# Attention input of a two-block transformer kernel: one joint stage with five gate tiles, three gate tiles in quarters

## The chip, the cores and the metric

The kernel runs on one core of a Trainium2 chip. Its engines each follow their own instruction list and meet only at semaphores: TensorE multiplies matrices (PE in the rows, PEld its weight loads), VectorE (DVE) and ScalarE (ACT) do elementwise work, GpSimd (POOL) a little, and SyncE (SP) issues the DMAs. A matmul writes into one of eight banks of PSUM (`ps`, "banks" in the rows); everything else lies in SBUF. The metric is device microseconds of one execution, median of the runs. Lower is better.

## The reference, cut to what matters

The function is a first block (two attentions, a mixture of 16384 experts) followed by a second block on 272 rows (16 meta tokens and 256 tokens), first attention, then a gated delta rule. The change touches only the attention of the second block. Its core is:

```python
def attention_mixer(h, norm_w, w_in, q_norm_w, k_norm_w, sinks, w_out):
    u = rms_norm(h, norm_w) @ w_in
    q, k, v, gate = jnp.split(u, [1024, 1152, 1280], axis=-1)   # then 1024 columns of gate
    q = rms_norm(q.reshape(B, L, 16, 64), q_norm_w)
    k = rms_norm(k.reshape(B, L, 2, 64), k_norm_w)
    v = v.reshape(B, L, 2, 64)
    o = banded_sink_attention(q, k, v, sinks)   # window 128, plus the 16 meta keys, plus a sink logit
    return (o * jax.nn.silu(gate)) @ w_out
```

All is float32. There are 272 rows (L), 16 query heads and 2 key heads of 64.

## The kernel before, in words

Weights are tiles of 128 x 1024 floats (512 KB), eight 128 x 128 chunks each, that stream through a ring of four slots. The list `plan` fixes their order; `load_tiles` lets SyncE load the next one as soon as VectorE has done with the tile four back. Each tile is split: ScalarE rounds it to a high part (`make_high`, L175), VectorE subtracts to get the low part (`make_low`, L187). There are two buffers of each, so parts of a tile can be made only when the tile two back is used. `tile_T` (L222, L226) multiplies a tile: 16 matmuls with the high part and 8 with the low part, all into one bank, 128 x 272. The names `early` and `end_early` mean that the first two tiles of a group are split in the stage before.

A stage is an `nc.Block` in which every engine has its own list. At its end all engines meet. Around the change the stages of `second_block` are, in order:

1. `project_T`: 11 tiles of the attention input, heads on partitions. Tiles 0 to 7 are the queries, 8 and 9 the keys, 10 the values. VectorE copies each from its bank.
2. `value_rows_stage`: three transposes give the values with tokens on partitions. The first two gate tiles are split here.
3. `head_norm_stage`: ScalarE squares the ten tiles, TensorE adds the squares per head ("gather", L1449), VectorE and ScalarE form the inverse root (L1462, L1443, and `newton`, L1408 to L1416), TensorE spreads it over the rows again ("spread", L1456), VectorE multiplies (L1764).
4. `meta_attention_stage`: the 16 meta rows attend to each other. It is one chain: scores (L1667), peaks, exponentials, scaling, turning (L1672), values (L1678), copy (L1705).
5. `sink_attention_stage`: 16 units (a unit is two heads of 128 query rows; units 0 to 7 have two key tiles, units 8 to 15 three). In step u TensorE does the scores of unit u+2 (L1512), then in steps 0 to 7 a whole gate tile, then the values of unit u-1 (L1539), then turns the weights of unit u (L1524). Per unit VectorE adds the bias, finds peaks and scales (L1567 to L1591), ScalarE exponentiates (L1608, L1611) and copies the turned weights (L1619, L1622), the gate (L1640) and the output (L1630). Two steps after the last gate tile ScalarE applies Silu to all eight gates at once (L1647).

The order is written out by hand: the Python loops emit each engine's list, and only the semaphores set when an instruction may start. After these comes the output projection (L2784) and the delta rule.

## Time and profile before

| what | value |
|---|---|
| median of 3 runs | 1849.21 us (1848.17 to 1852.97) |
| the profiled execution | 1853.29 us, its span 1851.5 us, mean granted clock 0.947 |
| TensorE busy | 1679.9 us, 91% of the span |
| VectorE, ScalarE busy | 65%, 48% |
| DMA | 124 GB/s on average |
| projection to output projection | 1210.50 to 1371.49 us of the span |

The span is what the trace covers; the profiled execution is 1.8 us longer. A row of the timeline gives the start, the length, the engine, the line, the operation and its tiles, how many instructions were merged, and in brackets the idle time ahead of the first and what ended it. Merged instructions of a row may overlap with the next row at their ends, so the distance of two starts tells more than a length. A matmul of plain float32 counts as two instructions on TensorE (x2). "PEclk" is the clock that TensorE was granted, in parts of 2.4 GHz.

### The profile page before, as it was taken

Reading aid. Unit: us, or ns where it says so; the run is one execution under the profiler, and the core shown is the slowest. Engines: PE = TensorE matmul, PEld = TensorE weight load, DVE = VectorE, ACT = ScalarE, POOL = GpSimd, SP = SyncE. Lnnn points to the kernel's source line nnn. Section 1 sums busy time; section 2 is a strip of 40 time slices with the busy share of each in tenths; the row PEclk is TensorE's granted clock in tenths of the full one; section 3 lists DMA queues with packets and bytes.
Section 4 is the critical chain, followed back from the end, with each engine's and each line's share of the span. In section 5 each row is a group of like instructions: output and inputs, shape, how many; then the busy total and the mean of one; then the engine's idle time right before and its main releaser. Section 6 shows DMA issues by size and latency. Waiting matters only on the chain. (4 is left out here: it accounts for less than half of the span.)

```text
span 1851.5 us, 34628 instructions
## 1 busy us (share of the span) xinstructions
PE 1679.9 (91%) x13270; PEld 1497.3 (81%) x13270; DVE 1199.9 (65%) x2104; ACT 894.8 (48%) x1568; POOL 69.9 (4%) x35
## 2 busy tenths in 40 slices
PE   5989988899999999989999999687987999899969
PEld 5978777899999999988888888584656888788857
DVE  3456654479989799996666666544644657655555
ACT  3335544244554666665666666432633644233323
POOL 0000000000000000000000000000000333100000
PEclk9979998999999999999999999896978999999989
DMA  5532143454555433335666666431112444200004
GB/s 174 170 123 81 57 137 119 145 170 159 182 172 176 129 115 115 115 115 184 193 192 194 192 194 193 135 126 36 56 46 68 149 155 141 92 3 3 3 17 143
DMA packets 63079, 230.05 MB, mean 124 GB/s; under 512 B 7008, under 2 KB 7264, under 8 KB 62832
## 3 DMA queue, kind: packets, MB, share of 16 engines
q1 hardware_dynamic: 62960, 228.39, 38.9%
q8 instruction: 83, 1.36, 0.3%
q14 instruction: 36, 0.29, 0.1%
HBM read 227.32 MB, written 1.05 MB: 123 GB/s over the span
## 5 line engine op out<-in xcount | busy, mean ns | idle before, releaser
L974 DVE TENSOR_TENSOR tile_low<-weights,tile_high 128x1024 fp32r<-128x1024 f32 x252 | 307.2, 1222 | 146.6 <-ACT tile_high L964 142.8
L964 ACT ACTIVATE tile_high<-weights 128x1024 fp32r<-128x1024 f32 x252 | 268.2, 1064 | 136.2 <-issue 136.2
L175 ACT ACTIVATE tile_high<-weights 128x1024 fp32r<-128x1024 f32 x169 | 177.7, 1057 | 273.8 <-PE banks L222 107.6
L187 DVE TENSOR_TENSOR tile_low<-weights,tile_high 128x1024 fp32r<-128x1024 f32 x146 | 179.7, 1237 | 187.9 <-ACT tile_high L175 152.2
L222 PE MATMUL banks<-parts,tile_high 128*128 128x272 f32 (+1 forms) x1904 | 268.1, 295 | 14.6 <-PEq L262 6.8
L1026 PE MATMUL banks<-parts,tile_high 128*128 128x256 f32 x2048 | 272.4, 286 | 7.1 <-PEq L900 7.1
L222 PEld LDWEIGHTS banks<-parts,tile_high 128*128 128x128 f32 x1904 | 249.2, 195 | 32.1 <-issue 25.1
L1026 PEld LDWEIGHTS banks<-parts,tile_high 128*128 128x128 f32 x2048 | 256.9, 193 | 7.3 <-issue 7.3
L1311 PE MATMUL banks<-tile_high,parts 128*128 128x512 f32 x1024 | 254.6, 391 | 4.6 <-ACT parts L1291 4.6
L1311 PEld LDWEIGHTS banks<-tile_high,parts 128*128 128x128 f32 x1024 | 193.3, 189 | 45.0 <-issue 4.8
L1031 PE MATMUL banks<-parts,tile_low 128*128 128x256 f32 x1024 | 148.6, 288 | 21.6 <-DVE tile_low L974 21.5
L1031 PEld LDWEIGHTS banks<-parts,tile_low 128*128 128x128 f32 x1024 | 132.8, 193 | 28.3 <-DVE tile_low L974 27.9
L226 PE MATMUL banks<-parts,tile_low 128*128 128x272 f32 (+1 forms) x952 | 138.5, 288 | 0.9 <-DVE tile_low L187 0.9
L1311 PE MATMUL banks<-tile_low,parts 128*128 128x512 f32 x512 | 137.5, 390 | 0.0
L226 PEld LDWEIGHTS banks<-parts,tile_low 128*128 128x128 f32 x952 | 127.5, 193 | 1.1 <-DVE tile_low L187 1.1
L1311 PEld LDWEIGHTS banks<-tile_low,parts 128*128 128x128 f32 x512 | 96.7, 189 | 20.2
L1102 ACT ACTIVATE rows<-rows,kept 128x128 f32<-128x128 f32 x256 | 80.5, 391 | 62.7 <-DVE rows L1181 62.7
L1081 ACT ACTIVATE big<-banks 128x256 f32 (+1 forms) x79 | 52.7, 667 | 120.2 <-PE banks L1031 120.2
L1291 ACT ACTIVATE parts<-big 128x256 fp32r (+1 forms) x128 | 88.4, 692 | 4.3 <-PEq L1007 4.3
L2784 PE MATMUL banks<-tile_high,parts 128*128 128x512 f32 (+1 forms) x288 | 77.6, 417 | 8.7 <-ACT tile_high L175 6.6
L1328 DVE TENSOR_TENSOR parts<-big,parts 128x256 fp32r<-128x256 f32 x128 | 81.1, 635 | 1.0 <-ACT parts L1291 1.0
L1181 DVE TENSOR_TENSOR rows<-const,kept 128x512 f32<-128x512 f32 x128 | 80.8, 685 | 0.0
(341 smaller groups left out, 2000.4 us busy)
## 6 DMA issues: line engine op xcount, KB each, us to landing
weights<-in_peer_u SPq DMA_DIRECT2D x128, 512.0 KB, 3.6
weights<-in_peer_v SPq DMA_DIRECT2D x128, 512.0 KB, 3.5
weights<-in_dn_in SPq DMA_DIRECT2D x49, 512.0 KB, 3.6
weights<-in_in_t SPq DMA_DIRECT2D x19, 512.0 KB, 3.6
weights<-in_attn_t SPq DMA_DIRECT2D x19, 512.0 KB, 3.6
weights<-in_in_m SPq DMA_DIRECT2D x16, 512.0 KB, 3.6
weights<-in_wq SPq DMA_DIRECT2D x16, 512.0 KB, 3.5
weights<-in_dn_out SPq DMA_DIRECT2D x16, 512.0 KB, 3.6
```

The lines of the kernel that those rows point to most:

```text
L175: k.nc.scalar.activation(k.high[:, m % 2, :], k.ring.view(n), ACT.Copy).then_inc(*k.high_made.up())
L187: unit.tensor_tensor(k.low[:, m % 2, :], k.ring.view(n), k.high[:, m % 2, :].bitcast(F32), ALU.subtract).then_inc(*k.low_made[engine].up())
L222: ins = nc.tensor.matmul(out, high[:, c, :], rhs(c)[part], start=part + c == 0, stop=False)
L226: ins = nc.tensor.matmul(out, low[:, c, :], rhs(c)[0], start=False, stop=c == chunks - 1)
L964: k.nc.scalar.activation(k.high[:, (s + j) % 2, :], k.ring.buf[:, j % RING, :], ACT.Copy).then_inc(k.high_made.sem, 1)
L974: k.nc.vector.tensor_tensor(k.low[:, (s + j) % 2, :], k.ring.buf[:, j % RING, :], k.high[:, (s + j) % 2, :].bitcast(F32), ALU.subtract).th ...
L1026: ins = nc.tensor.matmul(ps[:, bank, 0:S], high[:, c, :], x[:, c, :], start=part + c == 0, stop=False)
L1031: ins = nc.tensor.matmul(ps[:, bank, 0:S], low[:, c, :], k.pair(S)[0][:, c, :], start=False, stop=c == KC - 1)
L1181: return nc.vector.tensor_tensor(out, iota.unsqueeze(1).broadcast_to([P, Q, NKEY]), k.chosenT[:, o, Q * g:Q * g + Q].unsqueeze(2).broadcas ...
L1291: nc.scalar.activation(stage[:, j % STAGES, :], c_of(i, j), ACT.Copy).then_inc(staged.sem, 1)
L1311: ins = nc.tensor.matmul(ps[:, 2 * tt + half, :], c[:, j % STAGES, tt * P:tt * P + P], v[:, half, :], start=head and j + part == 0, stop=t ...
L1328: nc.vector.tensor_tensor(stage_low[:, j % STAGES, :], c_of(i, j), stage[:, j % STAGES, :].bitcast(F32), ALU.subtract).then_inc(staged_low ...
```

## The change

Stages 1 to 4 become one stage, `attn_in_stage`, with 16 tiles instead of 11: the eleven of before and the first five gate tiles (`GATES_FIRST`). Four banks take the tiles in turn. The gather of head tile t follows tile t+1; the value transposes follow tile 11, the spreads tile 12, the meta scores tile 13. Spreads use two banks in turn and one matmul of full width each, from a table `picks` that VectorE writes at the start. The turning and the values of the meta attention stand after tile 15. Gates are copied by ScalarE. The remaining three gate tiles go through `tile_piece`, six matmuls of a tile at a time, one piece in each of the steps 0 to 11 of the sink attention. The split of a tile then stands at steps 5, 9 and 13, the Silu at step 14 in place of 10.

```diff
-N_ATTN = 11
+N_ATTN, GATES_FIRST = 11, 5
...
+def tile_piece(pe, k, n, out, rhs, piece, pieces):
...
+    for m in range(3 * KC * piece // pieces, 3 * KC * (piece + 1) // pieces):
+        part, c = divmod(m, KC)
+        if m == 0:
+            await_high(pe, k, n)
+        if m == 2 * KC:
+            await_low(pe, k, n)
+        ins = nc.tensor.matmul(out, (low if part == 2 else high)[:, c, :], rhs(c)[part % 2], start=m == 0,
+                               stop=m == 3 * KC - 1, skip_group_check=True)
...
+def attn_in_stage(k):
...
+            def gather(c):
+                pe.wait_ge(*squared.at(c + 1))
+                nc.tensor.matmul(ps[0:HEADS, 7, 0:L], k.c("pair")[:, 18 - 2 * c:38 - 2 * c], sq[:, c % 2, :],
+                                 start=c == 0, stop=c == V - 1).then_inc(*summed.up())
...
+            def spread(c):
+                if c == 0:
+                    pe.wait_ge(*root.at(7))
+                if c >= 2:
+                    pe.wait_ge(*applied.at(c - 1))
+                nc.tensor.matmul(ps[:, 5 + c % 2, 0:L], halves(c), r[:, 2, :], start=True, stop=True).then_inc(*wide.up())
...
+            for t in range(count):
+                if t >= 4:
+                    if t - 4 <= V:
+                        pe.wait_ge(*evacuated.at(t - 3))
+                    else:
+                        pe.wait_ge(*gated.at(t - 4 - V))
+                tile_T(pe, k, first + t, bank(t), lambda c: (high[:, c, :], low[:, c, :]))
+                if 1 <= t <= V:
+                    gather(t - 1)
+                if t == N_ATTN:
+                    turn_values()
+                if t == spread_at:
+                    for c in range(V):
+                        spread(c)
+                if t == meta_at:
+                    meta_scores()
+            meta_turn()
+            meta_values()
...
+            for t in range(-AHEAD, count):
+                if 0 <= t <= V:
+                    evacuate(t)
+                if t == spread_at:
+                    for c in range(V):
+                        finish(c)
+                if t + AHEAD < count:
+                    make_low(dve, k, first + t + AHEAD)
+                if t == norm_at:
+                    mean_squares()
+                if t == N_ATTN:
+                    dve.wait_ge(*rooted.at(1))
+                    newton(nc, dve, root, r[:, 0, :], r[:, 1, :], r[:, 2, :], r[:, 3, :])
+                    copy_values()
+                if t == meta_at:
+                    meta_peaks()
+                if t == meta_at + 1:
+                    meta_scale()
+            for n in early(k, "attn_g"):
+                make_low(dve, k, n)
+            dve.wait_ge(*meta_product.at(2))
+            done(nc.vector.tensor_copy(over.rearrange("p h n -> p (h n)"), ps[0:m, 4, 0:AH * m]))
+            dve.wait_ge(*meta_product.at(3))
+            done(nc.vector.tensor_copy(k.y2[:, :, 0:m], ps[:, 7, 0:8 * m].rearrange("p (c n) -> p c n", c=8)))
...
+            for t in range(-AHEAD, count):
+                if t + AHEAD < count:
+                    make_high(act, k, first + t + AHEAD)
...
+                if t >= N_ATTN:
+                    act.wait_ge(k.ring.used.sem, first + t + 1)
+                    nc.scalar.activation(T[:, GATE + t - N_ATTN, :], bank(t), ACT.Copy).then_inc(*gated.up())
...
+            for n in early(k, "attn_g"):
+                make_high(act, k, n)
...
-                if u < fills:
-                    if u:
-                        pe.wait_ge(*gated.at(u))
-                    tile_T(pe, k, gate_tile(u), fill, lambda c: (high[:, c, :], low[:, c, :]))
+                if u < filled:
+                    if u and u % pieces == 0:
+                        pe.wait_ge(*gated.at(u // pieces))
+                    tile_piece(pe, k, gate_tile(u // pieces), fill, lambda c: (high[:, c, :], low[:, c, :]), u % pieces, pieces)
```

How the instruction lists move, at three places. First TensorE before, from the value transposes (L1723) through gathers (L1449), spreads (L1456) and the meta attention (L1667 to L1678) to the first scores of the sink attention (L1512):

```order
L1723 MATMUL banks<-const,big 128x128 x2
L1718 UNCONDITIONAL_BRANCH
L1445 UNCONDITIONAL_BRANCH
L1449 MATMUL banks<-big 20x272 x10
L1456 MATMUL banks<-big,const 64x272 x20
L1430 UNCONDITIONAL_BRANCH
L1663 UNCONDITIONAL_BRANCH
L1667 MATMUL banks<-big 16x16 x16
L1672 MATMUL banks<-const,rows 16x16 x16
L1678 MATMUL banks<-rows,big 64x16 x16
```

The same place now, from tile 11 on (value transposes L1477, spreads L1485, meta scores L1491, turning L1499, values L1507):

```order
L1477 MATMUL banks<-const,big 128x128 x2
L222 MATMUL banks<-parts,tile_high 128x272 x16
L226 MATMUL banks<-parts,tile_low 128x272 x8
L1485 MATMUL banks<-big 128x272 x10
L222 MATMUL banks<-parts,tile_high 128x272 x16
L226 MATMUL banks<-parts,tile_low 128x272 x8
L1491 MATMUL banks<-big 16x16 x16
L222 MATMUL banks<-parts,tile_high 128x272 x16
L226 MATMUL banks<-parts,tile_low 128x272 x8
L222 MATMUL banks<-parts,tile_high 128x272 x16
L226 MATMUL banks<-parts,tile_low 128x272 x8
L1499 MATMUL banks<-const,rows 16x16 x16
```

Four gate tiles moved in between the parts; the turning of the meta weights and their values have no tile behind them in this stage.

Second, VectorE at the end of the joint stage now: the last step of the meta scaling (L1574), the early low parts (L187), the copy of the turned weights (L1599), the copy of the meta output (L1601), and the bias of the sink attention (L1722):

```order
L1573 RECIPROCAL small<-small 16x16
L1574 TENSOR_TENSOR rows<-rows,small 16x256
L187 TENSOR_TENSOR tile_low<-weights,tile_high 128x1024 x2
L1599 COPY rows<-banks 16x256
L1601 COPY big<-banks 128x8x16
L1461 UNCONDITIONAL_BRANCH
L1712 UNCONDITIONAL_BRANCH
L1722 SCALAR_TENSOR_TENSOR big<-big,banks 128x144 x2
```

Before, the two early low parts stood ahead of the head norm, right after the value copies (L1729). Now they stand between the meta scaling and the copy that the meta values wait for.

Third, TensorE in the first steps of the sink attention before (turning L1524, scores L1512, values L1539):

```order
L222 MATMUL banks<-parts,tile_high 128x272 x16
L226 MATMUL banks<-parts,tile_low 128x272 x8
L1524 MATMUL banks<-const,big 16x128 x2
L1524 MATMUL banks<-const,big 128x128 x2
L1512 MATMUL banks<-big 128x144 x2
L222 MATMUL banks<-parts,tile_high 128x272 x16
L226 MATMUL banks<-parts,tile_low 128x272 x8
L1539 MATMUL banks<-big 64x128 x4
```

And now (piece L240, turning L1679, scores L1667, values L1694):

```order
L240 MATMUL banks<-parts,tile_high 128x272 x6
L1679 MATMUL banks<-const,big 16x128 x2
L1679 MATMUL banks<-const,big 128x128 x2
L1667 MATMUL banks<-big 128x144 x2
L240 MATMUL banks<-parts,tile_high 128x272 x6
L1694 MATMUL banks<-big 64x128 x4
```

Where 24 matmuls of a tile stood in a step, six stand.

## Rows read from the trace of the kernel before

**Rows 1.** The page, its first line.

```profile
span 1851.5 us, 34628 instructions
```

**Rows 2.** Stretches: us; busy PE, PEld, DVE, ACT, POOL; clock; DMA share, GB/s.

```profile
1260.50:1271.00 10.50, 9.33 (x40) 4.46 (x40) 5.44 (x11) 0.00 (x0) 0.00 (x0) 0.50 0.01 2
1281.00:1287.50 6.50, 6.33 (x30) 5.73 (x31) 3.56 (x16) 2.13 (x11) 0.00 (x0) 0.50 0.51 165
1342.40:1356.00 13.60, 11.87 (x45) 7.00 (x45) 6.59 (x24) 6.49 (x25) 0.00 (x0) 0.50 0.00 1
1369.80:1376.40 6.60, 4.91 (x12) 3.22 (x13) 4.00 (x6) 1.29 (x2) 0.00 (x0) 0.50 0.48 163
```

**Rows 3.** Timeline of TensorE, 1222 to 1281: start, length, idle before in brackets.

```profile
1222.57 2.16 PE L222 MATMUL banks<-parts,tile_high 128*128 128x272 f32 x16
...
1225.57 2.16 PE L222 MATMUL banks<-parts,tile_high 128*128 128x272 f32 x16
...
1244.53 0.49 PE L1723 MATMUL banks<-const,big 128*16 128x128 f32 x3 [0.80 <-PEq L329]
1248.82 7.59 PE L1449 MATMUL banks<-big 128*20 128x272 f32 x20 [3.81 <-ACT big L1441]
1260.99 9.33 PE L1456 MATMUL banks<-big,const 20*64 20x272 f32 x40 [4.58 <-DVE big L1416]
...
1275.76 0.59 PE L1672 MATMUL banks<-const,rows 16*16 16x16 f32 x16 [3.95 <-DVE rows L1701]
1276.92 3.19 PE L1678 MATMUL banks<-rows,big 16*64 16x16 f32 x32 [0.57 <-DVE rows L1703]
1281.04 2.31 PE L1512 MATMUL banks<-big 64*128 64x144 f32 x12 [0.93 <-PEq L1661]
```

**Rows 4.** Timeline of VectorE and ScalarE, 1228 to 1289.

```profile
1228.91 1.23 DVE L187 TENSOR_TENSOR tile_low<-weights,tile_high 128x1024 fp32r<-128x1024 f32 x1 [1.42 <-ACT tile_high L175]
...
1244.59 2.00 ACT L175 ACTIVATE tile_high<-weights 128x1024 fp32r<-128x1024 f32 x2 [6.71 <-PEq L329]
...
1257.37 1.84 DVE L1408 RECIPROCAL big<-big 20x272 f32<-20x272 f32 x1 [0.49 <-ACT big L1443]
...
1263.12 0.50 DVE L1764 SCALAR_TENSOR_TENSOR big<-banks,param,big 128x272 f32<-128x272 f32 x1 [0.34 <-PE banks L1456]
...
1285.34 0.50 DVE L1591 TENSOR_SCALAR big<-big,small 128x144 f32<-128x144 f32 x2
...
1288.59 0.40 ACT L1640 ACTIVATE big<-banks 128x272 f32<-128x272 f32 x1 [0.16 <-PE banks L226]
```

**Rows 5.** Timeline of TensorE in the delta input stage, gathers between tiles.

```profile
1441.09 0.63 PE L1846 MATMUL banks<-rows,big 128*16 128x272 f32 x2
...
1444.86 0.63 PE L1846 MATMUL banks<-rows,big 128*16 128x272 f32 x2
```

**Rows 6.** Timeline of TensorE in the sink attention and after it.

```profile
1306.23 2.26 PE L222 MATMUL banks<-parts,tile_high 128*128 128x272 f32 x16
...
1309.43 1.51 PE L1539 MATMUL banks<-big 16*64 16x128 f32 x8
...
1311.85 2.27 PE L222 MATMUL banks<-parts,tile_high 128*128 128x272 f32 x16
...
1333.43 1.95 PE L1539 MATMUL banks<-big 16*64 16x128 f32 x12 [0.43 <-ACT big L1622]
...
1336.07 0.73 PE L1512 MATMUL banks<-big 64*128 64x272 f32 x4
1337.23 1.95 PE L1539 MATMUL banks<-big 16*64 16x128 f32 x12 [0.43 <-ACT big L1622]
...
1344.13 3.39 PE L1539 MATMUL banks<-big 16*64 16x128 f32 x12 [3.54 <-ACT big L1622]
...
1350.04 3.39 PE L1539 MATMUL banks<-big 16*64 16x128 f32 x12
...
1371.49 5.21 PE L2784 MATMUL banks<-tile_high,parts 128*16 128x512 f32 x12 [2.19 <-ACT parts L2744]
```

More of the change, by code:

```diff
@@ L227, in tile_T @@
     tile_used(ins, k, n)
+def tile_piece(pe, k, n, out, rhs, piece, pieces):
+    nc = k.nc
+    high, low = parts(k, n, KC)
+    for m in range(3 * KC * piece // pieces, 3 * KC * (piece + 1) // pieces):
[6 more added lines that the diff above has]
+                               stop=m == 3 * KC - 1, skip_group_check=True)
+        if m == 2 * KC - 1:
+            ins.then_inc(*k.high_used.up())
+    if piece == pieces - 1:
+        tile_used(ins, k, n)
 def tile_used(ins, k, n):
@@ L1417, in newton @@
     dve.wait_ge(*sig.last())
-def head_norm_stage(k, chunks, heads, gather, spread, scale, eps, finish):
-    nc, ps, xs = k.nc, k.ps, chunks
-    n = len(xs)
-    squared, summed, vec, rooted, wide, applied = k.start("head_squared", "head_summed", "head_vector",
-                                                          "head_rooted", "head_spread", "head_applied")
-    sq = k.squares2
-    r = k.factors[0:heads]
+def attn_in_stage(k):
+    nc, ps, T = k.nc, k.ps, k.T2
+    AK, V, GATE, HEADS, m = 8, 10, 10, 20, META
+    first, count = k.tiles["attn_t"], N_ATTN + GATES_FIRST
+    evacuated, squared, summed, root, rooted = k.start("heads_evacuated", "head_squared", "head_summed", "head_vector",
+                                                       "head_rooted")
+    wide, applied, turned, copied, gated = k.start("head_spread", "head_applied", "values_turned", "values_copied",
+                                                   "gate_made")
+    meta_product, vec, exped = k.start("meta_product", "meta_vector", "meta_exped")
+    high, low = k.pair(L)
+    r, sq = k.factors[0:HEADS], k.squares2
+    bank = lambda t: ps[:, t % 4, 0:L]
+    spans = [(0, META)] + [(META + tt * P, P) for tt in range(NT)]
+    norm_at, spread_at, meta_at = N_ATTN - 1, N_ATTN + 1, N_ATTN + 2
+    halves = lambda c: k.picks[0:HEADS, P * c:P * c + P]
+    k.meta_soft, k.meta_turned = k.carve(k.mid, (AH, META), (AH, META))
+    soft, over = k.meta_soft[0:m], k.meta_turned[0:m]
+    st = k.small[0:m, 24:24 + 4 * AH].rearrange("p (a h) -> p a h", a=4)
+    across = lambda ap: ap.unsqueeze(2).broadcast_to([m, AH, m])
+    upto = k.tiles["attn_g"]
     with nc.Block() as block:
@@ L1480, in sink_attention_stage @@
     stored, stats, gated = k.start("att_stored", "att_stats", "gate_made")
-    fills = AH // 2
+    fills, pieces = KC - GATES_FIRST, 4
+    filled = fills * pieces
     gate_tile = lambda i: k.tiles["attn_g"] + i
-    ahead = [gate_tile(i) for i in range(AHEAD, fills)] + list(early(k, "attn_out"))
+    ahead = dict(zip(range(pieces + 1, 16, pieces), [gate_tile(i) for i in range(AHEAD, fills)] + list(early(k, "attn_out"))))
     high, low = k.pair(L)
     fill = ps[:, 7, 0:L]
-    value_bank = lambda u: 6 + u % 2 if u > fills else 6
+    value_bank = lambda u: 6 + u % 2 if u > filled else 6
     units = [(tt, a) for tt in range(NT) for a in range(AH // 2)]
@@ L1635, in _ @@
                     exps(u)
-                if 1 <= u <= len(ahead):
-                    make_high(act, k, ahead[u - 1])
-                if 1 <= u <= fills:
-                    act.wait_ge(k.ring.used.sem, gate_tile(u - 1) + 1)
-                    nc.scalar.activation(T[:, GATE + u - 1, :], fill, ACT.Copy).then_inc(*gated.up())
+                if u in ahead:
+                    make_high(act, k, ahead[u])
+                if u and u <= filled and u % pieces == 0:
+                    done = u // pieces
+                    act.wait_ge(k.ring.used.sem, gate_tile(done - 1) + 1)
+                    nc.scalar.activation(T[:, GATE + GATES_FIRST + done - 1, :], fill, ACT.Copy).then_inc(*gated.up())
                 if u >= 2:
@@ L1714, in value_rows_stage @@
-def value_rows_stage(k, spans, following):
-    nc, ps = k.nc, k.ps
-    turned, copied = k.start("values_turned", "values_copied")
-    with nc.Block() as block:
-        @block.tensor
-        def _(pe):
-            for i, (c0, n) in enumerate(spans):
-                nc.tensor.transpose(ps[0:n, i, 0:P], k.vT2[:, c0:c0 + n], k.ident).then_inc(*turned.up())
-        @block.vector
-        def _(dve):
-            for i, (_, n) in enumerate(spans):
-                dve.wait_ge(*turned.at(i + 1))
-                nc.vector.tensor_copy(k.v2[0:n, i, :], ps[0:n, i, 0:P]).then_inc(*copied.up())
-            for n in early(k, following):
-                make_low(dve, k, n)
-        @block.scalar
-        def _(act):
-            for n in early(k, following):
-                make_high(act, k, n)
+                    nc.scalar.activation(T[:, GATE:GATE + KC, :], T[:, GATE:GATE + KC, :], ACT.Silu).then_inc(*gated.up())
```

208 lines of the change are left out of this document (92 added, 116 removed).

## The prediction

> **What bounds the kernel now.** I began with the page: the kernel takes 1851.5 us of span on one core [rows 1]. TensorE is busy for 91% of it, so only work taken off TensorE's path, or idle or slow time closed on it, can pay. I then read the timeline of TensorE through the attention input. Eleven projection tiles run back to back, 3.00 us from start to start. After them TensorE mostly waits: 0.80 us before the value transposes, 3.81 before the ten gathers, 4.58 before the spreads, 3.95, 0.57 and 0.93 around the meta attention [rows 3]. That is 14.6 us in idle ahead of the rows shown. The reader is to see there five small stages, each a chain through ScalarE and VectorE with nothing beside it, between 1243.7 and 1281.04. A second cost lies in the stretches: at 1260.5 to 1271, and still at 1281 to 1287.5, the granted clock is 0.50, the 1.2 GHz level [rows 2]. The sink attention then holds eight gate tiles, one a step: a step takes 5.62 us, 3.20 of it the tile, and TensorE has no idle in it [rows 6]. Its later steps without a tile take 3.80, with 0.43 idle. One wait of 3.54 belongs to the Silu that runs on ScalarE between two steps.
>
> So the order is: TensorE bounds the steps with a tile, chains bound the middle, and the clock adds to both. DMA does not bound; a tile needs only to come every 3 us and did in the projection.
>
> **The change part by part.** I follow TensorE from 1210.50, where the projection starts in both versions, to the first matmul of the output projection, at 1371.49 before [rows 6].
>
> *The joint stage.* Twelve tiles (0 to 11) at 3.00 are 36.0. Ten gathers come between them. The nearest row is the same kind of matmul between two tiles in the delta input stage: from gather to gather 3.77, a tile within it, so 0.77 each, 7.7 together [rows 5]. With 0.1 for the start that gives 43.8. The gathers wait for nothing: the square of tile t has the whole of tile t+1 to be made in.
>
> Then VectorE decides. It splits tile 13 (1.23, starting 0.34 after tile 11 ends, as 1228.91 lies 0.34 behind the tile that began at 1225.57 and took 3.00) [rows 3, 4] and only then does the Newton step, 3.62 from its reciprocal to the first spread (1257.37 to 1260.99) [rows 3, 4]. With a small overlap the spreads can start 5.1 us after tile 11. TensorE fills 3.5 of that with the value transposes (0.5) and tile 12. The stall is 1.6.
>
> The ten spreads now have two banks and alternate with VectorE's 0.50 each [rows 4]. Before, they took 9.33 for ten at the 1.2 GHz level [rows 2, 3]. The bounds are 5.0 (VectorE alone) and 9.3. I take 6.3, since half of 9.3 is 4.7 and the hand-over between two engines adds a little to each 0.50.
>
> Tiles 13, 14 and 15 are 9.0, and the meta scores 0.6. The chain from meta scores to the weights took 4.6 (to 1275.76) [rows 3]; behind VectorE's split of tile 15 (1.2) it is 5.8 and fits within tiles 14 and 15. So tile 15 ends 21.0 after tile 11.
>
> The tail is where the change pays something back. ScalarE stands at tile 15's gate copy (0.40) and only then makes the two early high parts (2.00) [rows 4]. VectorE's two early low parts wait for them and are queued ahead of the copy of the turned meta weights, which TensorE waits for. The queue is 0.1 + 0.4 + 2.0, then 1.2 for the second low part, with the handovers 3.9; the copy adds 0.6. From the meta values to the next stage's first matmul it is 4.1 at the low clock (1276.92 to 1281.04) and 1.6 less at the high one [rows 3]. The tail is 8.6 or 7.0; I take 7.8.
>
> Sum: 43.8 + 5.1 + 6.3 + 9.6 + 7.8 = 72.6 against 70.54 before. I add 1 for a drop of the clock after the spreads (none or some 3; the spreads did not bring the clock back before, though TensorE was busy 9.33 of 10.5 [rows 2]). The stage ends 3.1 later than before, with five gate tiles already done.
>
> *The sink attention at full clock.* The first step has no tile to hide its chain: from the first scores to the scaled weights it took 4.8 (1281.04 to 1285.34 and 0.50) [rows 3, 4]; with the turning 5.0 at full clock. A quarter tile is 0.75 by the plain tile, and a tile between other matmuls costs 3.20 instead of 3.00 [rows 3, 6]; I take 0.95, all 0.20 of that paid by each piece (bounds 0.75 and 1.2). Then:
> - steps 1 to 5: 5.62 - 3.20 + 0.95 = 3.37 each, 16.9;
> - steps 6, 7: some 0.2 more for wider scores, 7.2; step 8, between the kinds: 3.8;
> - steps 9 to 11: 3.80 + 0.95 - 0.43 = 4.32, 13.0. The piece covers the 0.43 of idle, because it stands between turning and values;
> - steps 12, 13: 7.6.
>
> That is 53.5. The values of unit 13 start 1.1 later (the copy of the turned weights takes 1.1 to 1.2, 1336.07 to 1337.23), those of 14 after the Silu 6.90 on (1337.23 to 1344.13 before), the last 3.80 on, and the next stage 4.1 after that [rows 6]. Together 69.4 against 90.45 before: 21.05 less. Of this 16.0 are five tiles of 3.20, the rest clock that was low before and idle covered, less the bare first step.
>
> Does VectorE or ScalarE take over? The steps without a tile went through in 3.80, so both engines can do one of the wide units in that or less [rows 6]; the narrow units are smaller. The split of a tile (1.23) now comes once in four steps, and the two score banks let VectorE lag by a step. I cost it at nothing; without that slack it is up to 1.2 at three places, 3.7.
>
> *The clock.* The tail leaves TensorE idle for over 3 us, so the attention should start at 1.2 GHz, as before. It was 6.5 us low then, with full tiles; after the Silu, with small matmuls only, 13.6 [rows 2]. In between lies 10: half of it less what the bare first step hides, +3 (bounds 0 and 6). After the Silu the low clock costs 2.1 a step (5.91 instead of 3.80) [rows 6]; one step and the last values are left, +3.7 (bounds 0 and 6). The output projection starts low as before (6.6 us) [rows 2], no difference.
>
> In all +3.1 - 21.05 + 3 + 3.7 = -11.2. On the profiled execution's own 1853.29 (span 1851.5) that is 1842.1. The runs shown have a median of 1849.21, 4.1 below that execution, so I predict 1838.
>
> **The clock and the skill.** The rows show that TensorE busy with spreads of 20 rows, or with small matmuls of the attention, stays at 1.2 GHz for over 10 us [rows 2], while full tiles brought it back within 6.5. The Trainium skill, "TensorE: Matmul & The Clock Gate", section "A second HAM failure mode: psum-queue depth-cycling", says that TensorE can swing between its two levels when it idles briefly again and again between groups of matmuls; its Part 4 adds that transposes do not count as activity like matmuls. By that rule thin pieces would hold the clock worse than whole tiles, and the time would come out as in rival C; without it as in the forecast. This trace has steps of 3.80 with 0.43 idle at the high level, which speaks against a swing at the idle seen here.
>
> **The rivals.**
>
> A. The clock stays up: no drop after the spreads, the attention starts high. Stage +1.3, attention -21.05, Silu 0: about -20, so 1829. For it: TensorE has far less idle before the attention. Against: the tail's wait is as long as those that went before a drop.
>
> B. The joint stage gives back more. Spreads at 9.3 (+3), a clock drop of 3 more in tiles 13 to 15 (+2), tail 8.6 (+0.8), pieces of 1.1 (+1.8): -11.2 + 7.6 = about -4, so 1845. For it: the order puts VectorE's chain ahead of everything there. Against: the delta stage hides the same chain.
>
> C. The clock does not come back in the attention because the tile matmuls, which brought it back before, are cut to a quarter in each step. At 1.2 GHz steps 0 to 11 (45.9 us) take up to 36 more, since some of the first step is no matmul time; -11.2 - 3 + 36 = +22, so 1871. It makes the kernel slower once more than about 28 us of the attention are low (half of it outweighs 14.2). For it: 13.6 us low after the Silu with TensorE 87% busy. Against: it then rose with the same small matmuls, and even the steps without a tile held the high level.
>
> D. The change does not do what it says: a piece that waits for a gate copy, or a DMA not landed. ScalarE copies a gate a step before the next tile's first piece; I see no price and give it with B.
>
> **How the numbers follow.** Forecast 0.63, A 0.15, B (with D) 0.14, C 0.08. The forecast's own range is 1832 to 1843. With A inside and B at its edge the range for 8 in 10 is 1828 to 1846; it leaves out C and the tails. A measurement of this kernel tells about 0.3%, 5.5 us, from no change. Faster: 0.60 of the forecast, A and 0.03 of B: 0.78. Same: the rest of the forecast and of B, 0.14. Slower: C, 0.08.
>
> **What would show it.** In the new profile: tiles 3.8 apart while gathers run; one TensorE wait of about 1.6 before the first spread; spreads about 0.63 apart; a wait of over 3 us between meta transposes and meta values, ended by VectorE's copy; the attention starting near 1284 and its steps at 3.4, then 4.3. I am wrong if spreads are paced at 0.9 with the clock high, if steps with a piece take over 3.8 at full clock (VectorE or ScalarE bound), or if the granted clock is 0.50 through many of them.

## The result: 0.25% slower, against a forecast of 0.6% faster

The changed kernel takes 1855.8 us (median of 9 runs, 1853.2 to 1858.7), the kernel before 1851.2 in the same comparison. The ratio is 1.0025 with a 95% interval of 1.0015 to 1.0036. The forecast was 1838, with a range to 1846; both the size and the sign were wrong. The profiled execution took 1854.46 us.

The page's first line and four stretches of the trace follow, with the columns of [rows 2]: the granted clock is the third number from the right, 1.00 for 2.4 GHz and 0.50 for 1.2 GHz. The first stretch holds the spreads and tile 13, the second runs from the tail of the joint stage into the attention, the third is the rest of the attention up to the Silu, the last runs from the wait on the Silu into the output projection:

```profile
span 1852.7 us, 34568 instructions
```

```profile
1256.80:1271.70 14.90, 14.72 (x51) 10.40 (x53) 6.77 (x14) 1.06 (x1) 0.00 (x0) 0.54 0.09 35
1281.90:1312.70 30.80, 28.19 (x132) 19.46 (x132) 13.04 (x59) 10.65 (x43) 0.00 (x0) 0.50 0.09 35
1312.80:1356.90 44.10, 38.38 (x248) 24.43 (x246) 30.19 (x104) 29.74 (x89) 0.00 (x0) 1.00 0.04 13
1357.20:1374.00 16.80, 12.86 (x42) 8.06 (x43) 4.62 (x8) 3.42 (x7) 0.00 (x0) 0.50 0.17 62
```

In the first of these stretches the clock is almost all at 1.2 GHz (0.54), and so it is for 30.8 us around the attention's start. Then 44 us are high, with the same quarter tiles in the steps. In the rows below, "..." marks rows that are left out. The timeline of TensorE through the joint stage, answering [rows 3] and [rows 5]:

```profile
1240.53 0.64 PE L1471 MATMUL banks<-big 128*20 128x272 f32 x2
...
1244.30 0.64 PE L1471 MATMUL banks<-big 128*20 128x272 f32 x2
...
1251.75 0.49 PE L1477 MATMUL banks<-const,big 128*16 128x128 f32 x3
...
1256.84 9.09 PE L1485 MATMUL banks<-big 20*128 20x272 f32 x20 [1.60 <-DVE big L1434]
1265.86 4.00 PE L222 MATMUL banks<-parts,tile_high 128*128 128x272 f32 x16
1269.66 2.02 PE L226 MATMUL banks<-parts,tile_low 128*128 128x272 f32 x8
1271.60 0.57 PE L1491 MATMUL banks<-big 64*16 64x16 f32 x32
...
1278.30 0.55 PE L1499 MATMUL banks<-const,rows 16*16 16x16 f32 x16
1282.57 3.19 PE L1507 MATMUL banks<-rows,big 16*64 16x16 f32 x32 [3.72 <-DVE rows L1599]
1286.69 2.31 PE L1667 MATMUL banks<-big 64*128 64x144 f32 x12 [0.93 <-PEq L1461]
```

Gathers are 3.77 apart. The wait ahead of the spreads is 1.60. The spreads then take 9.02 from start to start, 0.9 each, and tile 13 takes 5.7 where a tile takes 3.0. The tail has the wait of 3.72 that ends with VectorE's copy L1599. The attention, answering [rows 6]; L1694 are the values, one row a step:

```profile
1300.78 2.54 PE L1694 MATMUL banks<-big 16*64 16x128 f32 x8
...
1306.64 2.54 PE L1694 MATMUL banks<-big 16*64 16x128 f32 x8
...
1330.48 1.95 PE L1694 MATMUL banks<-big 16*64 16x128 f32 x12
...
1334.72 1.95 PE L1694 MATMUL banks<-big 16*64 16x128 f32 x12
...
1357.87 3.39 PE L1694 MATMUL banks<-big 16*64 16x128 f32 x12 [4.20 <-ACT big L1777]
...
1363.73 3.39 PE L1694 MATMUL banks<-big 16*64 16x128 f32 x12 [1.09 <-ACT big L1777]
1369.30 5.08 PE L2834 MATMUL banks<-tile_high,parts 128*16 128x512 f32 x12 [2.18 <-ACT parts L2794]
```

A narrow step takes 5.86 at the low clock (1300.78 to 1306.64), a wide one 4.24 at the high clock. From the first projection tile (1207.96) to the output projection (1369.30) it is 161.34 us, where it was 160.99. So the part that was changed came out even. Behind it, in code that is the same, the trace takes 483.4 us to its end, where it took 480.0. These 3.4 us are most of the 4.6 between the medians. The part ahead of the projection differs between single executions too, by 2.5 us in these two traces (1207.96 and 1210.50), and was not looked into.

### The profile page after: what moved, and what is told of

Same layout as the page of the kernel before. It is cut to its first block and busy times, and to the rows that moved or that the text cites. A ratio compares the mean times of both kernels' runs of the same rounds, so it can differ in the third digit from the quotient of the medians.

```text
span 1852.7 us, 34568 instructions
## 1 busy us (share of the span) xinstructions
PE 1690.2 (91%) x13250; PEld 1504.5 (81%) x13250; DVE 1197.6 (65%) x2105; ACT 894.2 (48%) x1568; POOL 71.0 (4%) x35
## 5 line engine op out<-in xcount | busy, mean ns | idle before, releaser
L187 DVE TENSOR_TENSOR tile_low<-weights,tile_high 128x1024 fp32r<-128x1024 f32 x146 | 177.6, 1222 | 176.8 <-ACT tile_high L175 143.1
L222 PE MATMUL banks<-parts,tile_high 128*128 128x272 f32 (+1 forms) x1856 | 260.7, 294 | 15.1 <-PEq L280 7.4
L222 PEld LDWEIGHTS banks<-parts,tile_high 128*128 128x128 f32 x1856 | 241.7, 195 | 36.2 <-issue 25.4
L1044 PEld LDWEIGHTS banks<-parts,tile_high 128*128 128x128 f32 x2048 | 257.0, 194 | 7.3 <-issue 7.3
```

Of the source, the lines that this page charges most:

```text
L187: unit.tensor_tensor(k.low[:, m % 2, :], k.ring.view(n), k.high[:, m % 2, :].bitcast(F32), ALU.subtract).then_inc(*k.low_made[engine].up())
L222: ins = nc.tensor.matmul(out, high[:, c, :], rhs(c)[part], start=part + c == 0, stop=False)
L1044: ins = nc.tensor.matmul(ps[:, bank, 0:S], high[:, c, :], x[:, c, :], start=part + c == 0, stop=False)
```

## Experiments

Two theories stood first. T: the forecast's times at full clock hold, and the gain was lost to the granted clock, through the spreads and through thin work in the attention. Its rival: waits (1.6, 3.7 us and the bare first step) lose the time and drop the clock. All ratios are to the kernel before in the same comparison. In the code, "..." marks lines that are left out.

**Whole tiles in steps 0 to 2.**

```diff
-    fills, pieces = KC - GATES_FIRST, 4
+    fills, pieces = KC - GATES_FIRST, 1
...
```

The splits of the tiles that follow move with them, to steps 1 to 3; the Silu stays at step 14.

> The changed kernel, with its last three gate tiles whole in steps 0 to 2 of the sink attention instead of in twelve quarters; the Silu stays at step 14. Theory (thin pieces hold the clock down): the changed kernel was at 1.2 GHz from before the attention's start at 1286.7 until 1312.7 of its span, 26 us, where the kernel before, with whole tiles, was so for 6.7 us. With whole tiles it should be low for about 7 us, the stage 161.3 -> about 152 us, the kernel 8 to 10 us faster than the changed one, about 4 us faster than the kernel before. Rival (the bare first step and the longer tail hold it down, not the pieces): the low stretch stays at 20 us or more and the time within 3 us of the changed kernel's.

Measured: 1861.9, ratio 1.0052 (1.0037 to 1.0068), slower than the changed kernel. Both expectations were wrong. The clock was low for 10.2 us at the attention's start and later for 41 us more. Two stretches of its trace:

```profile
1291.00:1308.00 17.00, 16.14 (x116) 12.28 (x115) 12.01 (x44) 11.01 (x34) 0.00 (x0) 1.00 0.12 32
1308.50:1348.50 40.00, 39.90 (x147) 21.46 (x146) 20.85 (x78) 16.30 (x61) 0.00 (x0) 0.50 0.00 1
```

With whole tiles in the first steps the clock was up by 1291. It fell at 1307.9, 6 us after the last whole tile, and stayed down for 41 us, in which TensorE was busy 39.90 of 40.00 with the attention's small matmuls alone (64 rows or columns, 16 x 64, 128 x 16). So here a fully busy TensorE did not have the clock back for 40 us. That is no rule: in the same trace the clock rose at 1348.9 among such matmuls, and in the kernel before it did so at 1356.0, where the low stretch of [rows 2] ends. In the changed kernel, with a quarter tile in each step, it was high from 1312.6 through the same steps, so over the whole attention the quarters did better: 82.6 us from the first scores to the output projection against 89.3. How long the clock is low at the start is not settled by the attention's code: with the same code it was 31 us in the changed kernel and 13.6 and 13.7 in the next two experiments.

**Spreads in pairs between fifths of tile 13.**

```diff
+                        spread(2 * i)
+                        spread(2 * i + 1)
+                        tile_piece(pe, k, first + t, bank(t), lambda c: (high[:, c, :], low[:, c, :]), i, 5)
```

> The changed kernel, with the ten spreads put in pairs ahead of the five fifths of tile 13 instead of all ten after tile 12. Theory (a burst of matmuls with 20 rows drops the clock): the clock stays at 2.4 GHz through tile 13; spreads and tile 13 take about 9.5 us instead of 15.1 (9.0 + 6.0), the kernel about 5 us faster than the changed one. Rival (the 1.6 us wait ahead of the spreads drops it): the clock falls in the same place, spreads and tile take 15 us or a little more, no gain. A third reading, that the hand-over between TensorE and VectorE paces the spreads at 0.9 whatever the clock, would show spreads 0.9 apart at a granted clock of 1.0.

Measured: 1853.3, ratio 1.0000 (0.9987 to 1.0013). The clock fell in the same place, and spreads and tile took 16.5 us. That matches the rival's account of this place, but the next experiment denies its reason. The joint stage came out 3.9 us longer than in the changed kernel and the attention 7.3 shorter, because its low stretch was 13.6 us and not 31; that is why the kernel is a little faster all the same.

**The Newton step ahead of the split of tile 13.**

```diff
+                if t == N_ATTN:
+                    dve.wait_ge(*rooted.at(1))
+                    newton(nc, dve, root, r[:, 0, :], r[:, 1, :], r[:, 2, :], r[:, 3, :])
                 if t + AHEAD < count:
                     make_low(dve, k, first + t + AHEAD)
...
```

> The changed kernel, with VectorE's Newton step ahead of the split of tile 13 instead of behind it, so that TensorE need not wait 1.6 us before the spreads. Theory (the burst of 20-row matmuls drops the clock): the wait is gone, 1.6 us less, and the clock still falls during the spreads, which still take about 9 us or a little less. Rival (the wait drops the clock): the clock stays at 2.4 GHz, spreads 6.3 us and tile 13 3.0, in all 6 to 7 us less.

TensorE's timeline at the spreads and the first group of tile 13:

```profile
1259.54 8.47 PE L1485 MATMUL banks<-big 20*128 20x272 f32 x20
1267.94 4.00 PE L222 MATMUL banks<-parts,tile_high 128*128 128x272 f32 x16
```

There is no wait ahead of the spreads any more, and they still take 8.47, and tile 13 still starts at half speed: its first group takes 4.00 instead of 2.16. The clock falls at 1262.3, 2.8 us after the first spread. So the wait is not what drops the clock. The kernel took 1844.4, ratio 0.9968 (0.9947 to 0.9988), with one run at 1864.7: more than the 1.6 us, because the attention's low stretch was 13.7 us in this trace.

**The splits out of the meta chain's way.**

```diff
-            for n in early(k, "attn_g"):
-                make_low(dve, k, n)
+            make_low(dve, k, upto)
             dve.wait_ge(*meta_product.at(2))
             done(nc.vector.tensor_copy(over.rearrange("p h n -> p (h n)"), ps[0:m, 4, 0:AH * m]))
+            make_low(dve, k, upto + 1)
...
```

ScalarE makes both high parts ahead of the gate copy of tile 15 as well.

> The changed kernel, with the split of the first two later gate tiles moved out of the meta chain's way: ScalarE makes both high parts before it copies the gate of tile 15, VectorE makes one low part before the copy of the turned meta weights and one behind it. Theory: the tail from the meta transposes to the attention's first scores, 8.4 us in the changed kernel (1278.3 to 1286.7), becomes about 5, so 3.5 us less; the clock in the attention stays low as before because that is the pieces' doing. Rival (the wait of 3.7 us in the tail is what makes the attention start low and stay low): the low stretch also shrinks by 10 us or more, and the gain is 8 us or more.

Measured: 1857.0 (1841.5 to 1858.7), ratio 1.0011 (0.9995 to 1.0028). The tail did shrink, from 8.4 to 3.75 us (1280.63 to 1284.38). The attention was then low for 37.6 us in the profiled execution, as the row of this stretch shows:

```profile
1284.50:1322.00 37.50, 36.50 (x142) 23.09 (x142) 18.80 (x80) 14.57 (x59) 0.00 (x0) 0.50 0.12 43
```

The time saved was lost again to the clock: the attention took 87.5 us instead of 82.6. So a tail without the long wait does not shorten the low stretch, and both expectations missed that it could grow. One run of the twelve took 1841.5 where most took 1857; no trace shows what the clock did in it.

**Filling matmuls.** They are full-size (128 x 128 by 272), unused, and stand where TensorE waits: the 24 in the wait of 3.7 us of the tail, the eight, which take 1.9 us, where it waited 0.87 ahead of the first turning.

```diff
+                pe.wait_ge(*gated.at(3))
+                warm(1, 24)
...
+                if u == 0:
+                    for _ in range(8):
+                        nc.tensor.matmul(ps[:, 6, 0:L], high[:, 0, 0:P], high[:, 1, :], start=True, stop=True)
```

> The changed kernel, with 24 more full-size matmuls (128 x 128 by 272, their result unused) in TensorE's wait of 3.7 us between the meta transposes and the meta values, and 8 in the first step of the sink attention ahead of the first turning. Theory (what TensorE does in the tail decides whether the attention starts at 2.4 GHz, and once it is up it stays up with quarter tiles, as it did from 1313 on): the clock is high at the attention's start or within 7 us of it, against 26 us low in the changed kernel; 8 to 10 us faster than the changed kernel. Rival (steps with a quarter tile cannot hold or regain the clock): it falls again within the narrow units, 20 us or more of it low, no gain.

> The changed kernel, with only the eight filling matmuls in the first step of the attention, not the 24 in the meta wait. Theory (near the attention's start a little full-size work decides whether the clock comes up, and the quarter tiles then hold it): low until about 1296 instead of 1313, 6 to 8 us faster than the changed kernel. Rival (the clock has to be high through the tail already): 15 us or more low from the start, gain under 3 us.

Both: 1846.5, ratio 0.9970 (0.9959 to 0.9981). The eight in the first step alone: 1836.1, ratio 0.9906 (0.9890 to 0.9921). In the trace with both, the clock is low for 6.8 us at the attention's start, as its theory had it, and the gain over the changed kernel is 9.3 us (8 to 10 expected). Two stretches of the one with eight:

```profile
1283.00:1293.20 10.20, 8.19 (x57) 7.49 (x58) 5.08 (x21) 2.00 (x10) 0.00 (x0) 0.51 0.30 103
1293.40:1345.00 51.60, 49.06 (x317) 31.69 (x317) 37.77 (x141) 33.27 (x113) 0.00 (x0) 1.00 0.04 11
```

Once up, the clock held through all quarter-tile steps until the Silu. The eight matmuls, 1.9 us of work, shortened the attention by 8.4 us (82.6 to 74.2), a little above the 6 to 8 that were expected. The median fell by 19.7, though, and the other half of it is not their doing in any way that was shown: it lies behind the output projection's start, in unchanged code. These rows of the output projection's first matmuls, in the kernel with both fillings and in the one with eight, show it:

```profile
1359.04 5.15 PE L2843 MATMUL banks<-tile_high,parts 128*16 128x512 f32 x12 [2.18 <-ACT parts L2803]
```

```profile
1362.26 4.26 PE L2837 MATMUL banks<-tile_high,parts 128*16 128x512 f32 x12 [2.18 <-ACT parts L2797]
```

The first kernel takes 150.95 us from its first tile (1208.09) to this row and 483.5 from there to the end of its span of 1842.6. The second takes 152.92 (from 1209.34) and 474.8 (span 1837.1). So the 24 in the tail did help, by 2.0 us in the changed part, and the kernel with eight is faster only by what the clock does later: it is low for 16.6 us instead of 21.9 in the stage of the output projection, and for 24.8 instead of 38.4 in the delta stage.

**Filling behind the spreads.** Two of the same behind each spread.

> The changed kernel, with two more full-size matmuls (result unused) behind each of the ten spreads. They cost 2.5 us at most at full clock, part of it in time that TensorE waits for VectorE anyway. Theory (the spreads drop the clock because they use 20 of the 128 rows): the clock stays at 2.4 GHz in spreads and tile 13, spreads and tile take 8 + 3 = 11 us instead of 15.1, 4 us faster. Rival (the 1.6 us wait before them drops it): low as before, spreads and tile take 15 + 4 = 19 us, 4 us slower.

Measured: 1858.4, ratio 1.0032 (1.0014 to 1.0051). The clock fell in the spreads all the same; spreads and tile took 23 us, more than either expectation. Two full-size matmuls beside each spread did not hold it.

**Spreads over 128 rows.** The same ten matmuls, with zeros in rows 20 to 127 of both operands.

```diff
-    halves = lambda c: k.picks[0:HEADS, P * c:P * c + P]
+    halves = lambda c: k.picks[:, P * c:P * c + P]
...
-                nc.tensor.matmul(ps[:, 5 + c % 2, 0:L], halves(c), r[:, 2, :], start=True, stop=True).then_inc(*wide.up())
+                nc.tensor.matmul(ps[:, 5 + c % 2, 0:L], halves(c), k.factors[:, 2, :], start=True, stop=True).then_inc(*wide.up())
...
```

> The changed kernel, with the spreads over all 128 rows: the table and the vector of factors are padded with zeros in rows 20 to 127, the same ten matmuls of the same length otherwise. Theory (the spreads drop the clock because they work on 20 rows): the clock stays at 2.4 GHz through spreads and tile 13, 9.1 + 6.0 become about 6.3 + 3.0, so up to 5.5 us less than the changed kernel. Rival (the small share of time in which TensorE streams between the hand-overs to VectorE, whatever the rows): the clock falls in the same place, no difference.

TensorE's timeline at the spreads and tile 13 of the padded kernel, and then two stretches of its trace:

```profile
1256.73 6.47 PE L1485 MATMUL banks<-big 128*128 128x272 f32 x20 [1.60 <-DVE big L1434]
1262.83 2.37 PE L222 MATMUL banks<-parts,tile_high 128*128 128x272 f32 x16
1265.04 1.16 PE L226 MATMUL banks<-parts,tile_low 128*128 128x272 f32 x8
```

```profile
1256.70:1275.00 18.30, 16.11 (x140) 13.15 (x140) 11.30 (x26) 5.61 (x9) 0.00 (x0) 1.00 0.18 58
1286.00:1342.00 56.00, 50.78 (x328) 32.68 (x328) 38.45 (x144) 38.09 (x121) 0.00 (x0) 1.00 0.04 11
```

This is the plainest result of the study. The wait of 1.60 and the hand-overs are as in the changed kernel; on TensorE only the rows differ. The clock is 1.00 through spreads and tiles, the spreads take 6.10 from start to start where the forecast had 6.3, tile 13 takes 3.3. In all ten traces of the changed lists with spreads over 20 rows the clock falls 1.0 to 6.1 us after the first spread begins. In the three with padded spreads (this one and two below) it stays up until the tail, 18 us or more behind the first spread. The joint stage takes 73.4 us (1207.82 to 1281.22), 5.3 less than in the changed kernel, against "up to 5.5" in the expectation. The kernel took 1841.9, ratio 0.9941 (0.9922 to 0.9960), 14 us less than the changed kernel. That is more than the padded place can give: in the trace the attention is 8.8 us shorter as well, with a low stretch of 10.2 us at its start instead of 31, and the part behind it 3.0.

**All together.** First without padding but with filling behind the spreads, then with padding, then with 36 more filling matmuls in the wait on the Silu.

> All of it together: the Newton step ahead of the split of tile 13, two filling matmuls behind each spread, the early splits out of the meta chain's way, four filling matmuls in the rest of that wait and eight in the first step of the attention. Theory (the gain that was forecast was lost to the clock, everything else went as worked out): the clock is high from the projection to the Silu; stage about 161.3 - 4 (spreads, tile 13) - 1.6 - 3.5 - 9 = 143 us, the kernel about 1837, 15 us faster than the kernel before. Rival (thin steps fall to the low clock by themselves): the stage stays at 150 us or more, 1845 or more.

> The padded spreads, the Newton step first, the early splits out of the way, four filling matmuls in the rest of the meta wait and eight in the first step of the attention; no filling behind the spreads. If the padding holds the clock: stage about 141 us, the kernel 1838 or less. If it does not: about the 1843 of the kernel with all edits so far, less the 2.5 us that its filling behind the spreads cost.

> The combined kernel, with 36 more filling matmuls in TensorE's wait of 4.2 us on the Silu. Theory (what the Silu costs beyond its own wait is the clock that falls in it): the last values, the turning and the start of the output projection run at 2.4 GHz, 5 to 6 us less than the combined kernel without it. Rival (the wait alone costs, the later low stretch comes from the short gaps at the stage's end): no gain, or a loss of up to 1 us.

Measured: 1842.8, ratio 0.9943 (0.9924 to 0.9963); 1832.5, ratio 0.9883 (0.9864 to 0.9902); 1833.2, ratio 0.9886 (0.9867 to 0.9905). In the first, without padding, the changed part takes 151.0 us, the rival's 150 or more. The second, with padding, takes 140.7 where 141 was expected, and is the best version, 1.2% faster than the kernel before. Here is its clock in the joint stage and in the attention:

```profile
1253.00:1274.00 21.00, 19.34 (x186) 16.28 (x185) 14.81 (x30) 7.18 (x11) 0.00 (x0) 0.99 0.23 76
1281.50:1331.00 49.50, 46.96 (x303) 29.96 (x302) 35.46 (x131) 31.98 (x110) 0.00 (x0) 1.00 0.03 12
```

Filling the Silu's wait gained nothing, and the expectation of 5 to 6 us failed. TensorE's row of the 36 filling matmuls, behind the row of the values after the Silu in the kernel without them:

```profile
1337.51 3.38 PE L1703 MATMUL banks<-big 16*64 16x128 f32 x12 [3.04 <-ACT big L1789]
```

```profile
1337.95 5.18 PE L1697 MATMUL banks<-parts 128*128 128x272 f32 x36
```

The wait was only 3.04 us there, and the filling takes 5.18, since the clock is still low when it begins. From the turning ahead of it to the values it is 6.2 us instead of 4.5. The last two values then run at full speed and give 2.0 back, and the output projection's first tile is slow again. So this run does not test whether a filling that fits the wait would pay.

**Where the time lies.** Start to start in the traces, in us: the joint stage (first tile to first scores), the attention (to the output projection's first matmul) and all that lies behind, which no edit here touches.

| kernel | joint stage | attention | behind | median |
|---|---|---|---|---|
| before | 70.5 | 90.5 | 480.0 | 1851.2 |
| changed | 78.7 | 82.6 | 483.4 | 1855.8 |
| Newton step first | 76.0 | 75.2 | 483.3 | 1844.4 |
| 24 and 8 filling | 77.4 | 73.6 | 483.5 | 1846.5 |
| 8 filling | 78.7 | 74.2 | 474.8 | 1836.1 |
| padded spreads | 73.4 | 73.8 | 480.4 | 1841.9 |
| all, padded | 67.2 | 73.5 | 483.4 | 1832.5 |

**The delta stage.** What was left is the 3 to 4 us behind the attention.

> The kernel before, unchanged, for a second trace. In the changed kernel and its four variants so far the later delta stage had 10 us of low clock near 1740 to 1750 and came out 3 to 5 us later relative to the output projection than in the one trace of the kernel before. If that is chance of one execution, this trace shows the low stretch too; if it belongs to the change, it does not.

The second trace of the kernel before has no low stretch there either; this row of the first shows the place:

```profile
1742.00:1753.00 11.00, 11.00 (x259) 10.46 (x258) 4.05 (x7) 4.01 (x6) 0.00 (x0) 1.00 0.01 3
```

Of the 12 traces with the changed lists so far, 11 have one of about 10 us; the kernel with eight filling matmuls in the first step alone has none. Was it the change, or the moment? One idle reciprocal moves the stage:

```diff
+            delayed, = k.start("d_delayed")
+            for _ in range(1):
+                nc.vector.reciprocal(flat(k.ET)[:, 0:P], k.c("ones")).then_inc(*delayed.up())
+                dve.wait_ge(*delayed.last())
             spread_gates(0)
```

> The kernel before, with one idle reciprocal of 128 x 128 on VectorE ahead of the delta rule's first product, so that the delta stage starts about 0.9 us later and is otherwise untouched. Theory (the 10 us of low clock that the changed kernel and nearly all its variants show late in the delta stage, worth 5 us, come from the moment at which the stage's marginal spots meet the clock, not from the change's code): a shift in the kernel before can bring them as well, so low stretches in that stage differ from the kernel before and the time moves by more than 0.9 us. Rival (they belong to something that the change does): no new low stretch, 0.9 us slower.

> The same with two such reciprocals, about 1.8 us. Theory: again other low stretches than in the kernel before are possible, the time off by something other than 1.8 us. Rival: 1.8 us slower, low stretches as before.

> The changed kernel with one such reciprocal, about 0.9 us. The changed kernel's delta stage starts 1.3 us earlier behind the output projection than in the kernel before, so this puts it back to nearly the same distance. Theory (the moment decides): the low stretch late in the delta stage goes, 4 us or more less than the changed kernel in spite of the delay. Rival: it stays, 0.9 us slower.

Kernel before with one: 1857.4, ratio 1.0025 (1.0015 to 1.0035). With two: 1856.9, ratio 1.0026 (1.0012 to 1.0040). Changed kernel with one: 1850.8, ratio 0.9998 (0.9986 to 1.0009), 5.0 us less than without. The same piece of the stage in the changed kernel, in the kernel before with one, and in the changed kernel with one:

```profile
1737.90:1749.00 11.10, 11.04 (x130) 10.26 (x132) 4.08 (x12) 2.65 (x3) 0.00 (x0) 0.56 0.01 1
```

```profile
1745.00:1756.00 11.00, 11.00 (x130) 10.17 (x126) 3.45 (x9) 2.64 (x3) 0.00 (x0) 0.53 0.01 1
```

```profile
1735.00:1747.00 12.00, 11.52 (x261) 10.87 (x262) 6.54 (x17) 3.73 (x5) 0.00 (x0) 1.00 0.01 3
```

A delay that measures 1.0 us in the traces makes the kernel before 5 us slower and the changed kernel 5 us faster. The low stretch comes and goes with it, in these traces; the changed kernel's delta stage takes 245.1 us with the delay, as in the kernel before, and 249.7 without. In the kernel before with one, the clock is also low for 7 us more near 1610 and for 3.4 near 1705, and the traced execution is one of the slowest of its twelve. The kernel before with two has no low stretch near 1750; it has 3.4 us more of low clock near 1610 and is 3.5 us later behind the output projection, 2.0 of it the delay. By its trace it did nearly what the rival said, and 3.5 does not quite make up the 4.8 of its ratio. So one shift of a microsecond changed in which spots the clock fell, in the code of before as in the changed one, and another hardly did. That every run of a kernel does what its one trace shows is not shown.

## Why the prediction was wrong

**The times at full clock were right.** Gathers 0.77 each, as forecast. The stall ahead of the spreads 1.60, forecast 1.6. Spreads 6.1 where the clock held, forecast 6.3. The tail's queue on VectorE, wait 3.72, was there and in that order. A narrow step with a piece 3.38 at full clock (forecast 3.37), a wide one 4.24 (4.32), two wide steps without one 3.80 each. The low clock after the Silu, which the forecast did count, cost 3.5 us, forecast 3.7. VectorE and ScalarE took nothing over, but for one wait of 0.53 on VectorE near the end of the attention. With the clock kept up through the spreads (zero-padded kernel) the joint stage took 73.4 us; the forecast without its 1 us for a drop was 72.6, and the tail accounts for 0.6 of the difference.

**The step that failed is the price of the low clock: the term of 3 us in the step headed "The clock", and the 1 us for a drop after the spreads.** The mechanism of the gain was right, and these two terms were sized too small. From the spreads' start to the meta scores the low clock cost 9.0 - 6.3 for the spreads and 5.7 - 3.0 for tile 13, 5.4 us instead of 1. The tail took 8.4 instead of 7.8. In the attention I took 10 us low and 3 us of cost, bounds 0 and 6. The clock was low from before its start for another 26 us and cost 9.4: 0.8 in the first step, 7.5 in the next three, 1.1 in the fourth. Above the forecast that is 4.4 + 0.6 + 6.4 = 11.4, and with the 149.8 forecast for the stage it makes 161.2; measured were 161.3.

**Why I mis-sized it.** I had a row that warned of it: TensorE was busy 9.33 of 10.5 us with spreads and stayed at 0.50 [rows 2]. That row does not show that spreads drop the clock, since it was low already when they began; but it gave no ground either to price a drop by a burst of such matmuls among full tiles with 1 us, a third of what I put as its bound. Rival C, with a chance of 0.08, had the place right, the steps with quarter tiles. Its reason holds for the start alone: with whole tiles the clock was back after 10 us instead of 31, and once up it held through the quarters. I took its price as all or nothing, 28 us of low clock to turn the sign. Low clock for 26 us, 16 more than forecast, cost 6.4 us more than priced, over half of the forecast gain of 11.2; the spreads and the tail took the rest. The Trainium skill, "TensorE: Matmul & The Clock Gate", section "What's actually happening", ties the clock to how busy TensorE has been. The traces here do not follow the busy time of the rows: at 39.90 of 40.00 us with small matmuls the clock stayed at 0.50, and through ten spreads with 108 more rows of zeros it stayed at 1.00, where through the same spreads without them it fell.

**The sign** came from the delta stage, which I had not looked at: in its trace the changed kernel has 10 us more of low clock there, and a delay of 1 us ahead of the stage takes them and 5 us away. No step of the prediction covered that a shift of an unchanged stage has a price. With that delay the changed kernel is even with the kernel before (0.9998).

What stays open: what makes the clock fall at the attention's start. It was low there in every trace, for 6.8 us at the least, with the tail's long wait and without it, and no run kept it up. The runs show how long it lasts with each edit, 6.8 to 38 us, and not why. It is open too whether every spot where the unchanged code behind is slow follows from the moment alone, and why runs of a kernel differ in the clock before 1160 us.

## What to carry to other kernels

Merging stages removes waits, but look at what is left on TensorE in each stretch. Here bursts on 20 rows went with a falling clock even when the engine was fully busy, and padding the contraction with zeros held it in all three traces, at 6.10 us for ten spreads instead of 9.02. Before pricing a gain from a trace with clock changes, price the stage at both levels and give the low one a real chance. When a small change moves the total by a few us, compare time and clock of the unchanged stages too, and shift them by a microsecond before believing the sign. This goes for the gains as well: half of what eight filling matmuls seemed to bring lay in code that they did not touch.

## What the runs showed of the hardware

When VectorE and GpSimd both subtract at once, the one that starts second takes longer, and a small shift decides which it is. In the delta input stage of the kernel before, both split a tile, GpSimd first:

```profile
1538.92 2.39 POOL L187 TENSOR_TENSOR tile_low<-weights,tile_high 128x1024 fp32r<-128x1024 f32 x1 [3.32 <-ACT tile_high L175]
1539.20 3.19 DVE L187 TENSOR_TENSOR tile_low<-weights,tile_high 128x1024 fp32r<-128x1024 f32 x1
```

In the changed kernel both start at the same recorded time:

```profile
1536.63 1.22 DVE L187 TENSOR_TENSOR tile_low<-weights,tile_high 128x1024 fp32r<-128x1024 f32 x1
1536.63 3.48 POOL L187 TENSOR_TENSOR tile_low<-weights,tile_high 128x1024 fp32r<-128x1024 f32 x1 [3.60 <-ACT tile_high L175]
```

VectorE's split takes 3.19 in one and 1.22 in the other, GpSimd's 2.39 and 3.48; 1.22 and about 2.4 are what each takes elsewhere in these stages. TensorE waited 0.90 for the slow one on VectorE, and the next tile starts 5.01 us after the one before instead of 3.84. These 1.2 us are most of the 1.3 by which the delta stage starts earlier behind the output projection in the changed kernel. They come close to the delay of 1.0 that took its low stretch away.
